# A decoder step on one core: the sums of the S5 scan's turned inputs go from VectorE to Pool

## What is computed

```python
bu_re = jnp.einsum('gph,blgh->blgp', bbar_re, ug)
bu_im = jnp.einsum('gph,blgh->blgp', bbar_im, ug)
elems = (jnp.broadcast_to(abar_re, shp), jnp.broadcast_to(abar_im, shp), bu_re, bu_im)
_, _, s_re, s_im = lax.associative_scan(_complex_affine_combine, elems, axis=1)
y = (jnp.einsum('ghp,blgp->blgh', c_re, s_re) - jnp.einsum('ghp,blgp->blgh', c_im, s_im) + d * ug)
```

## Time and profile before

| what | value |
|---|---|
| timed runs, median of 3 | 2292.18 us (2287.33 to 2307.16) |
| the profiled execution, first to last instruction | 2181.2 us |
| TensorE, VectorE, ScalarE, Pool busy | 1271.5, 1402.0, 428.4, 1060.0 us |
| scan loop in that execution | 122 to 330 us |

### The profile page before, as it was taken

One profiled execution on the slowest core, in us unless ns is written; L12 is line 12 of the kernel. 1 busy time (PEld: TensorE's weight loads), 2 busy tenths in 40 slices (PEclk: granted clock), 3 DMA queues, 4 the chain that ended last, 5 costly groups with the idle time before them and its releaser, 6 DMA issues.

```text
span 2181.2 us, 20941 instructions
## 1 busy us (share of the span) xinstructions
PE 1271.5 (58%) x6676; PEld 757.3 (35%) x6676; DVE 1402.0 (64%) x3356; ACT 428.4 (20%) x901; POOL 1060.0 (49%) x1103
## 2 busy tenths in 40 slices
PE   5987898767668756368737575853223533222234
PEld 3854566654556434245414333531000100000000
DVE  3679991342677645378887667567767677767630
ACT  4112342301233311233320011211010101101000
POOL 1012221000336644347676566576757677767664
PEclk9889899788889877688868887986666655666556
DMA  9154464205779999899999999999989999999987
GB/s 294 48 182 166 136 213 138 79 9 215 255 278 394 396 401 321 318 324 405 403 404 400 397 387 405 394 383 409 410 326 410 383 410 410 409 410 409 403 348 284
DMA packets 260328, 696.11 MB, mean 319 GB/s; under 512 B 23743, under 2 KB 109847, under 8 KB 259119
## 3 DMA queue, kind: packets, MB, share of 16 engines
q0 software_dynamic: 149760, 545.33, 63.4%
q1 hardware_dynamic: 109346, 148.91, 20.3%
q10 hardware_dynamic: 1112, 0.53, 0.1%
HBM read 685.74 MB, written 9.08 MB: 319 GB/s over the span
## 4 chain that ended last, share of the span: by engine, by line
DMA 27%; POOL 12%; DVE 12%; PE 9%; issue 8%; ACT 2%; SPq 2%; DVEq 1%; POOLq 0%; ACTq 0%
DMA arena<-in_expert_up_dram,rows 15%; DMA arena<-in_expert_down_dram,expert 6%; POOL arena L1857 6%; POOL arena L1837 6%; DVE arena L2544 5%; DMA arena<-in_state_ssm_dram 5%; PE ps L2198 4%; PE ps L2230 2%; SPq L1699 1%; DVE arena L2591 1%; DMA arena<-in_w_branch_b_dram 1%; PE ps L2206 1%; DVEq L2485 1%; ACT arena L1903 1%; PE ps L2416 1%
## 5 line engine op out<-in xcount | busy, mean ns | idle before, releaser
L2544 DVE CUSTOM_DVE_ANT_0 arena<-arena,ps 128x1024 f32<-128x1024 f32 x512 | 610.3, 1219 | 246.2 <-DMA arena<-in_expert_down_dram,expert 236.1
L2198 PE MATMUL ps<-arena 128*32 128x512 f32 x2048 | 364.7, 846 | 604.8 <-DMA arena<-in_expert_up_dram,rows 597.0
L1837 POOL DMA_INDIRECT arena<-in_expert_down_dram,expert x512 | 491.4, 960 | 320.1 <-issue 139.8
L1857 POOL DMA_INDIRECT arena<-in_expert_up_dram,rows x512 | 487.5, 952 | 286.1 <-issue 147.6
L2230 PE MATMUL ps<-arena 128*128 128x264 f32 (+1 forms) x1344 | 344.5, 417 | 87.7 <-ACT arena L1933 31.6
L2198 PEld LDWEIGHTS ps<-arena 128*32 128x32 f32 x2048 | 74.8, 136 | 828.6 <-issue 819.9
L2230 PEld LDWEIGHTS ps<-arena 128*128 128x128 f32 x1344 | 273.8, 208 | 164.2 <-ACT arena L1933 33.7
L714 PE MATMUL ps<-arena 128*128 128x256 f32 x640 | 162.6, 411 | 3.5 <-ACT arena L544 3.5
L714 PEld LDWEIGHTS ps<-arena 128*128 128x128 f32 x640 | 128.7, 206 | 46.8 <-issue 27.3
L463 POOL TENSOR_TENSOR arena<-arena 128x512 f32<-128x512 f32 x16 | 23.1, 1442 | 243.2 <-DVE arena L1057 243.2
L1877 ACT ACTIVATE arena<-arena 128x8 f32<-128x8 f32 x65 | 13.5, 208 | 598.8 <-DVE arena L2544 598.5
(11 more groups left out here) (456 smaller groups left out, 1823.9 us busy)
## 6 DMA issues: line engine op xcount, KB each, us to landing
arena<-in_w_in_dram SPq DMA_DIRECT2D x42, 1024.0 KB, 8.2
arena<-in_w_ada_dram SPq DMA_DIRECT2D x32, 512.0 KB, 5.7
arena<-in_w_query_dram SPq DMA_DIRECT2D x16, 1024.0 KB, 17.4
arena<-in_w_ada_dram SPq DMA_DIRECT2D x8, 1024.0 KB, 19.5
arena<-in_w_ada_final_dram SPq DMA_DIRECT2D x16, 512.0 KB, 4.0
arena<-in_w_out_dram SPq DMA_DIRECT2D x8, 1024.0 KB, 18.5
arena<-in_expert_down_dram,expert POOLq DMA_INDIRECT x512, 12.2
arena<-in_expert_up_dram,rows POOLq DMA_INDIRECT x512, 11.9
```

Of the source, the lines that this page charges most:

```text
L1837: G.indirect_dma_start(U[i], None, down, bass.IndirectOffsetOnAxis(ap=at, axis=0))\
L1857: G.indirect_dma_start(Vr[r][j], None, up, bass.IndirectOffsetOnAxis(ap=at, axis=0))\
L2198: last = mm(ps[32 * j:32 * j + 32, c, :], Z[:, j, m, :], Vr[r][4 * half + j][:, c * 512:(c + 1) * 512], start=(p % 4 == 0 and m == 0), sto ...
L2544: V.tensor_tensor_reduce(U[i], U[i], row, 1.0, 0.0, ALU.mult, ALU.add, dots[n % 2][:, j:j + 1]).then_inc(s_uused, 1)
```

## The change

The two sums of a pass's turned input leave VectorE. Pool makes them in place (`turned(i)`: `prod[0] += prod[1]`, `prod[2] -= prod[3]`) as soon as the products are there, and the scans read them from `prod` and write `wr`, `wi`. The products of pass i+1 are written ahead: the first set stands before the loop, and each later one directly behind the second scans of the pass before, ahead of that pass's outputs. Pool's queue has the sums of pass i+1 ahead of the state of pass i. On TensorE, `bu(p+1)` stands ahead of the projection tiles of pass 2p+1 and no longer behind the first of them. Four semaphores are new.

```diff
@@ Pool
+            def turned(i):
+
+                pool.wait_ge(s_buread, i + 1)
+                G.tensor_tensor(prod[0], prod[0], prod[1], ALU.add).then_inc(s_wr, 1)
+                G.tensor_tensor(prod[2], prod[2], prod[3], ALU.subtract).then_inc(s_wi, 1)
+
             done = 0
+            turned(0)
             for i in range(NS5):
                 sr, si = S_of(i)
+                if i + 1 < NS5:
+                    turned(i + 1)
                 pool.wait_ge(s_part, i + 1)
@@ TensorE
                 if p:
                     y(p - 1)
-                some = loop_tiles(2 * p + 1)
-                for n in some[0:1]:
-                    proj(n)
                 if p + 1 < NS5 // 2:
                     bu(p + 1)
-                for n in some[1:]:
+                for n in loop_tiles(2 * p + 1):
                     proj(n)
@@ VectorE
-            for i in range(NS5):
+            wr, wi = wk[0], wk[1]
+            t1, t2, t3, t4 = prod
+            q1, q2, q3, q4 = part
+
+            def tables(i):
+                return (z[:, i:i + 1, :].to_broadcast([P, 2, TB5]) for z in (RC, RS))
+
+            def products(i):
+
                 br, bi = (ps[:, 2 * (i % 2) + j, :].rearrange("p (a b) -> p a b", a=2) for j in range(2))
-                c, s = (z[:, i:i + 1, :].to_broadcast([P, 2, TB5]) for z in (RC, RS))
-                wr, wi = wk[0], wk[1]
-                t1, t2, t3, t4 = prod
-                q1, q2, q3, q4 = part
+                c, s = tables(i)
                 dve.wait_ge(s_bu, i + 1)
                 if i:
-                    dve.wait_ge(s_part, i)
-
+                    dve.wait_ge(s_scan, 2 * i)
                 tt(t1, br, c, ALU.mult)
                 tt(t2, bi, s, ALU.mult)
                 tt(t3, bi, c, ALU.mult)
                 tt(t4, br, s, ALU.mult).then_inc(s_buread, 1)
-                dve.wait_ge(s_buread, i + 1)
-                tt(wr, t1, t2, ALU.add)
-                link(tt(wi, t3, t4, ALU.subtract))
-
+
+            products(0)
+            for i in range(NS5):
+                c, s = tables(i)
                 magb = PT[:, V_MAG, i:i + 1].to_broadcast([P, TB5])
                 ec, es = PT[:, V_COS + NLEV - 1, i:i + 1], PT[:, V_SIN + NLEV - 1, i:i + 1]
-                V.tensor_tensor_scan(wr[:, 0, :], magb, wr[:, 0, :], 0.0, ALU.mult, ALU.add)
-                link(V.tensor_tensor_scan(wi[:, 0, :], magb, wi[:, 0, :], 0.0, ALU.mult, ALU.add))
+                if i:
+                    dve.wait_ge(s_part, i)
+                dve.wait_ge(s_wr, i + 1)
+                V.tensor_tensor_scan(wr[:, 0, :], magb, t1[:, 0, :], 0.0, ALU.mult, ALU.add).then_inc(s_in, 1)
+                dve.wait_ge(s_wi, i + 1)
+                V.tensor_tensor_scan(wi[:, 0, :], magb, t3[:, 0, :], 0.0, ALU.mult, ALU.add).then_inc(s_in, 1)
+                dve.wait_ge(s_in, 2 * i + 2)
...
-                V.tensor_tensor_scan(wr[:, 1, :], magb, wr[:, 1, :], o[2], ALU.mult, ALU.add)
-                link(V.tensor_tensor_scan(wi[:, 1, :], magb, wi[:, 1, :], o[3], ALU.mult, ALU.add))
-
+                V.tensor_tensor_scan(wr[:, 1, :], magb, t1[:, 1, :], o[2], ALU.mult, ALU.add).then_inc(s_scan, 1)
+                V.tensor_tensor_scan(wi[:, 1, :], magb, t3[:, 1, :], o[3], ALU.mult, ALU.add).then_inc(s_scan, 1)
+                if i + 1 < NS5:
+                    products(i + 1)
+                dve.wait_ge(s_scan, 2 * i + 2)
                 if i:
                     dve.wait_ge(s_sr, i)
                     dve.wait_ge(s_S, i)
```

More of the change, by code:

```diff
@@ L314, in stage_front @@
     s_bu, s_buread, s_S, s_part, s_sr = sem("s5_bu"), sem("s5_buread"), sem("s5_S"), sem("s5_part"), sem("s5_sr")
+    s_in, s_wr, s_wi, s_scan = sem("s5_in"), sem("s5_wr"), sem("s5_wi"), sem("s5_scan")
     s_y, s_yread, s_ysamp, s_gelu = sem("s5_y"), sem("s5_yread"), sem("s5_ysamp"), sem("s5_gelu")
```

## The result

The changed kernel takes 2305.0 us (median of 20 runs, 2295.19 to 2320.49), the kernel before in the same comparison 2294.28 us (2270.72 to 2312.35, but for one run of 4157.73 us). The medians lie 10.7 us apart; the ratio of the fast runs, which leaves that one run out, is 1.0063 with a 95% interval of 1.0039 to 1.0086: slower by 14 us, between 9 and 20. The forecast was +12 us.

The account below looks back on a forecast made before the run. VectorE (DVE) was taken to bound the scan loop. Terms -23.0 + 32.1 + 2.4 + 0.5 = +12.0 us took the timed median of 2292.18 us to 2304 us, range 2289 to 2316.

Parts of the forecast that it names:

- Sums off DVE: Scan loop: without the two sums and the wait ahead, VectorE saves 1.44 us a pass, 23.0 us over 16 passes.
- Stops: VectorE's second and third outputs each lose 1.07 us to a Pool sum: 30 stops, +32.1 us, between 26.7 and 37.8.
- First pass: Start of the loop: Pool's sums have nothing to hide behind and the first scan is stopped, +2.4 us.
- Bias sums: Pool's four bias sums in the loop: three covered by the readout line, one stops a scan, +0.5 us.
- TensorE's order: Input transform ahead of one projection tile in the loop: TensorE has reserve, so the order costs nothing.
- The shift of the loop's end at full value: Behind the loop: loads, readout and z tiles wait for its end, so its whole shift counts in the kernel's time.
- The base: Timed median 2292.18 us, some 111 us above the profiled span; the same difference added to 2193 us gives 2304 us.
- Rival A: Outputs run freely beside Pool, no stop: -18 us, TensorE's idle time as floor, 2274 us; chance 0.08.
- Rival B: The 12 us shift vanishes behind the loop in the expert stage, where loads are busiest: no change, 2292 us; chance 0.07.
- Rival C: TensorE becomes the loop's bound through tiles at the 1.2 GHz level: 2322 us if 24 are slow; chance 0.05.

Follow-up runs that it names:

- products_ahead: Changed kernel with the two sums back on VectorE directly ahead of the scans, only the new order kept; ratio 0.9987 to the kernel before.
- pool_memset: Changed kernel with Pool writing zeros into the two tiles instead of forming the two sums; ratio 0.9920 to the kernel before.
- transform_behind: Changed kernel with TensorE's input transform back behind the first projection tile of pass 2p+1; ratio 1.0081 to the kernel before.
- outputs_first_dve: Changed kernel with outputs ahead of the next products, both sums back on VectorE, Pool's state sums beside the products; 2163.34 us, ratio 0.9911 to the kernel before.

## Why the prediction was right

Its mechanism held, and its size: 1.07 us a stop was forecast from a step of half the length (its terms add up to 1.08), and the outputs show 1757 - 685 = 1.07 us (the pitch from the second to the third output, 1.69 us against 0.60, gives 1.09). The pass was to grow to 13.56 us and has 13.60. The first and the fourth output, the lengths of Pool's new sums (1.6 to 1.75 forecast, 1.65 and 1.71 measured) and the convolution came out as written. The load of the GLU weights left at 336.5 us in the first profile and 337.9 in the second, where 338 to 339 was said; counted from the first product that is 12.8 to 12.9 us later than before. That the median of 2305.0 us lies 1 us from the 2304 forecast is in part luck: the measured difference is known only to between 9 and 20 us.

Step by step:

- **Sums off DVE, 23.0 us.** Right within 1 us. products_ahead shows its parts: two sums at 0.605 us, and 0.18 us for waits that the new order covers. It is 1.39 us a pass in place of 1.44, 22.2 us in all.
- **Stops, +32.1 us.** Right; pool_memset takes them away and ends 32 us below the changed kernel, as an estimate from the two ratios (0.9920 against 1.0067, each beside the kernel before on its own chip, 0.0147 x 2186 us; some 1 us of that belongs to the first pass). The outputs give 15 x 2.15 = 32.2 us.
- **First pass, +2.4 us.** Right. DVE waited 1.39 us for Pool and the first scan took 1.74 us (`122.92 1.74 DVE L1054`). From the first product to the end of the second scan the changed kernel needs 125.25 - 119.04 = 6.21 us, before it was 5.13, so 1.08 us where 1.0 was worked out.
- **Bias sums, +0.5 us.** The first scan beside the one of pass 2 took 1.21 us in place of 0.68; behind the others the readout covered them. Right.
- **TensorE's order, 0.** Right (transform_behind). DVE never waited for it behind the first pass. The forecast that TensorE's wait for DVE grows by about 12 us was wrong: it went from 19.9 us to 12.4 at the input transform and 8.9 at the readout, 21.3 in all (23.3 in the first profile). Of the 12.8 us by which the loop grew, TensorE was busy for 4.5 (177.1 before, 181.6 now), with a granted clock of 0.86 in the loop where it was 0.90, and waited 6.2 for ScalarE. No term of the sum rested on it.
- **The shift of the loop's end at full value.** Here the working was thin. The loop's end shifts by 12.9 us and the expert stage by 13.8 to 15.8 us from the same start. I hadn't seen that the last pass gets short (its products stand in the pass before) and that TensorE then waits for ScalarE. The effect is 1 to 3 us, as much as two profiles of one kernel differ, and what share of it is that wait is not shown.
- **The base.** "Some 111 us above that span (start and end around the program)" was wrong. In a run with its own profile the two are 1.7 us apart (2320.49 and 2318.8; 2202.72 and 2201.0). The sentence ahead of the prediction that puts the larger timed figure down to what lies around the span is wrong for the same reason. The 111 us are read as the difference between the chip that was profiled and the one that was timed: on the chips of the experiments the kernel before has medians of 2185 to 2187 us, near its profile's 2181.2. It did no harm only because a difference was added to the median, and the difference arises ahead of the expert stage.

Rival A (2274 us, no stop) is what pool_memset is: 18.6 us below the kernel before, where A had 18. Its floor was too high, though: TensorE was to give back no more than its 19.9 us of waiting, and the loop is 21.0 us shorter in pool_memset and 24.2 us in outputs_first_dve, where TensorE is busy for 164.8 us instead of 177.1, at a granted clock of 0.93. Rival B is out, since the shift arrived at the expert stage and in the ratio. Rival C is out, since the products never waited; its premise came true in part, the clock fell from 0.90 to 0.86.

## What to carry to other kernels

Before work goes to Pool, look at what VectorE does at that moment: a Pool sum that reads SBUF (1.27 us by itself) cost VectorE 0.89 to 1.07 us here when VectorE's operation has two SBUF inputs, and nothing when one of them comes from PSUM. Here two sums of 0.6 us on VectorE were traded for two stops of 1.07. The better change was to leave the sums and to turn the order, so that the Pool sums that exist fall on the operations with a PSUM operand: 2.0 us a pass (12.85 to 10.89), a ratio of 0.9911, without moving any work.

## What the runs showed of the hardware

- VectorE's queue, issued without a gap, doesn't keep Pool out. Pool gets its turn about at the end of the operation that is running (its sum of 1.65 us from 171.35 on leaves the undisturbed 1.27 us to begin at 171.73, by estimate, and the output that was running is recorded to 171.86), the next VectorE operation stands still, and then they alternate: each sum of 128x512 takes 1.27 us alone or beside PSUM operands, 1.44 beside 256-wide steps and 1.59 to 1.71 beside 512-wide ones; the difference is read as its own wait. The Trainium skill's page "SBUF — State Buffer" (section "Who interferes with whom") has this as a lock held for a whole instruction. By that rule, the trace agrees in both directions: outputs of 1.76 us behind a Pool sum, and Pool sums of 1.65 us behind an output.
- Scans are stopped too (1.74 us for 0.68), and a memset by Pool, which only writes, stops nothing (0.68 us beside it). The same section states the second for an instruction that only writes, and pool_memset shows it.
- Times differ by 5% for the same kernel: the kernel before took 2294 us in the main comparison and 2185 to 2187 us on the three chips of the experiments. That the chip is the reason is inferred; nothing else is known to have differed. Of the 117.8 us between the two profiles of the changed kernel, 117.3 lie behind the start of the expert stage (1753.1 us in the first, 1635.8 in the second).
